# Expert rows of a mixture-of-experts stage moved through DRAM instead of through selection matmuls

## The chip, the cores and the metric

The kernel runs on one core of a Trainium2 chip. The metric is the device time of one execution in microseconds (us); lower is better. TensorE (PE, with its weight load PEld), VectorE (DVE), ScalarE (ACT), GpSimd (POOL) and SyncE (SP) run their own instruction streams and meet at semaphores. SP and POOL also issue DMAs, all of which run on the same 16 DMA engines.

## What is computed

Two layers of a hybrid model on 256 tokens of 1,024 features, in f32. Layer 0 ends in a dense feed-forward block, layer 1 in a mixture of eight experts with two chosen per token, and the output is a last RMS norm. What matters here is the expert part:

```python
def moe_swiglu(h, w_router, w1, w3, w2):
    logits = (h @ w_router).astype(jnp.float32)
    top_v, top_i = lax.top_k(logits, TOP_K)            # 2 of 8
    gates = jax.nn.softmax(top_v, axis=-1)
    combine = jnp.sum(one_hot(top_i, N_EXPERTS) * gates[..., None], axis=-2)
    out = jnp.zeros_like(h)
    for e in range(N_EXPERTS):
        out = out + combine[..., e:e + 1] * swiglu(h, w1[e], w3[e], w2[e])   # D=1024, F=3584
    return out
```

## The kernel before

All large products take each f32 weight as a high and a low part. SP loads weight tiles of 1 MB into a ring of six slots (L911). ACT copies a tile to its high part `wh` (L429), DVE subtracts to get the low part `wl` (L433), and TensorE multiplies three combinations of high and low parts (L369 for the up projections w1 and w3, L394 for the down projection w2). `wh` and `wl` have three buffers. SP may refill a slot when DVE has split it: it waits on `w_split` in `free` and walks the program in order.

In the expert part the router picks two experts per token. Each chosen pair (token, expert) gets a slot number; an expert's pairs fill blocks of 128 slots, and each block is a job. Here there are 8 jobs, known only at run time, so each engine runs a loop over jobs. A job has 14 steps (pairs of 128 hidden columns). A step is a first up half, the turn of the last step's gated values (L382), a second up half, and the down product of the step before: three stages of 12 matmuls, 3 MB of weights. A job thus reads 42 tiles, 44.04 MB. `pe_steps`, `act_steps`, `dve_steps` and `sp_ffn` hold the stages of the four engines.

A job's input columns are picked by matmul. POOL builds 0/1 matrices `sel` from compares of slot numbers by DVE (`hit`, L844 and L891), and TensorE multiplies the rows of h by them (`gather`, through L1082, 32 matmuls in f32 halves). ACT and DVE split the result into `xh` and `xl` (L740, L829). The results of a job are in banks 2 and 3; ACT copies them to `yj` (L751), and TensorE multiplies them by the transposed gate matrix `pgt` (`turn_gates`, `scatter`), DVE adds the four banks to `xT` (L836), and the accumulators are zeroed again (`zero_acc`, L421). All this stands around a job's last down product and the next job's first up halves. The last norm works on feature-major `xT`: squares on ACT, sums by matmul, root, scaling on DVE, turning back by TensorE, four copies, one store of 1 MB (L994).

The order on each engine is the order in which the code is written. POOL's share in layer 0 is a chain for another mixer, which ends with a signal and is followed by a wait for `chunk_masked` before twelve maskings (L1075).

Of the kernel before, what the change touches and what calls it, by code (L numbers as in the profile page):

```python
# [21 lines left out]
F32 = mybir.dt.float32  # L22
# [23 lines left out]
C = P  # L46
# [99 lines left out]
def program(nc, A, out):  # L146
    ctx = ExitStack()
    with ctx:
# [35 lines left out]
        xl = sb("xl", [P, KT, T], F32R)  # L184
        proj = mx_sb("proj", [P, 26, T])
# [53 lines left out]
        sel = sb("sel", [P, TT, C])  # L239
        selg = sb("selg", [P, TT, C])  # L240
        selt = sb("selt", [P, TT, C])
        hit = sb("hit", [P, 2, TT, C])
        pgt = sb("pgt", [P, T])
        rt = sb("rt", [P, T])
        jt = sb("jt", [P, 2 * MAXJOBS], I32)
        idx = sb("idx", [P, 16], U32)

# [100 lines left out]
        SCATTER = (2, 3, 5, 6)  # L348
# [36 lines left out]
        def pe_down(pe, run, m, last=False):  # L385
# [4 lines left out]
            for o in range(2 if run.moe else KT):  # L390
                for a in range(2):
                    for g, b in ((gh, 0), (gh, 1), (gl, 0)):
                        if run.moe:
                            ins = nc.tensor.matmul(bank[2 + o][:], g[:, a, 0:C], w[b][:, a, o * 512:(o + 1) * 512],  # L394
                                                   start=False, stop=False, skip_group_check=True)
# [8 lines left out]
        def pe_steps(pe, run):  # L404

            def step(m, par):
                pe_up(pe, run, m, par, 0)
                pe_turn_gated(pe, run, m - 1)
                pe_up(pe, run, m, par, 1)
                pe_down(pe, run, m - 1)  # L410

            n = run.pairs - 1
            with pe.Fori(0, n // 2) as i:
                step(2 * i + 1, 1)
                step(2 * i + 2, 0)
            if n % 2:
                step(n, 1)
# [231 lines left out]

        def hrows():  # L650
            return wide[:].rearrange("p (a b) t -> p a (b t)", a=TT)

        def pe_moe(pe, mm, turn):
# [20 lines left out]
            pe.wait_ge(sem("h_copied"), 4)  # L674
# [11 lines left out]
            def turn_gates(j):  # L686
                pe.wait_ge(sem("selg_built"), j + 1)
                for tt in range(TT):
                    turn(bank[7][:, tt * P:(tt + 1) * P], selg[:, tt], sig="gates_turned" if tt else None)

            def scatter(j):

                pe.wait_ge(sem("gates_copied"), j + 1)
                pe.wait_ge(sem("acc_copied"), 2 * j + 2)
                for b in range(4):
                    for k in range(2):
                        dt = 2 * b + k
                        mm(bank[SCATTER[b]][:, k * T:(k + 1) * T], yj[:, dt * P:(dt + 1) * P], pgt[:],
                           sig="scattered" if k else None)
# [3 lines left out]
            zero_acc((2, 3))  # L703
            run = job(0)
            pe.wait_ge(sem("x_split"), x_before(1, 2) + 2)
# [4 lines left out]
            with pe.Fori(1, n_jobs) as j:  # L710
# [3 lines left out]
                turn_gates(j - 1)  # L714
# [4 lines left out]
                scatter(j - 1)  # L719
                pe.wait_ge(sem("scatter_added"), 4 * (j - 1) + 2)  # L720
                zero_acc((2, 3))
                pe_steps(pe, nxt)
# [3 lines left out]
            turn_gates(j)  # L726
            pe_down(pe, run, last, True)
            scatter(j)

        def act_moe(act, copy, f, square):  # L730
            for b in range(4):
                act.wait_ge(sem("h_turned"), b + 1)
                copy(hrows()[:, :, b * T:(b + 1) * T], bank[b][:].rearrange("p (a t) -> p a t", a=TT), "h_copied")
            act.wait_ge(sem("gate_logit"), 1)
# [9 lines left out]
            def gates(j):  # L744
                act.wait_ge(sem("gates_turned"), j + 1)
                nc.scalar.copy(pgt[:], bank[7][:, 0:T]).then_inc(sem("gates_copied"), 1)

            def acc(j):
                act.wait_ge(sem("stage_used"), job(j).down(0, True)[0] + 1)
# [1226 lines left out]
```

## Time and profile before

| | |
|---|---|
| runs of the kernel | 1789.15 us median of 3 (1787.06 to 1795.26) |
| the profiled execution | 1791.82 us |
| its span, first to last instruction | 1789.7 us |
| mean granted TensorE clock | 0.953 |
| PE, PEld, DVE, ACT, POOL busy | 94%, 80%, 75%, 59%, 6% of the span |
| bytes read from HBM | 426.25 MB |

The span is what the trace shows; the execution's own time is 2.1 us longer. The layers' mixers and the dense block take the first 745 us, the expert jobs run from 762 to 1771 us, and the rest is the end. A row of the page's groups gives an instruction's line, engine, operation, tiles written and read, count, busy time and mean duration.

### The profile page before, as it was taken

The page shows a single profiled execution, that of the slowest core. Times are in us where ns is not written, and L with a number is a line of the kernel's source. Part 1 is how long each engine was busy: PE and PEld are TensorE (multiplying, and loading weights), DVE is VectorE, ACT ScalarE, POOL GpSimd, SP SyncE. Part 2 cuts the span into 40 slices and gives each one's busy share as a digit, 9 for nine tenths or more (in the row PEclk, how much of TensorE's full clock was granted, in tenths as well). Part 3 has the DMA queues.
Part 4 walks back from the last instruction along what each step waited for, and adds up shares of the span by engine and source line. Part 5 has one row for each costly group of instructions (what it writes and reads, how often), then busy time and mean ns, then how long its engine had stood idle before and what let it go on. Part 6 is the DMA issues. An engine that isn't in the chain of part 4 may idle for free.

```text
span 1789.7 us, 27022 instructions
## 1 busy us (share of the span) xinstructions
PE 1677.0 (94%) x9570; PEld 1429.4 (80%) x9570; DVE 1347.3 (75%) x1286; ACT 1061.1 (59%) x1039; POOL 113.7 (6%) x151
## 2 busy tenths in 40 slices
PE   6889888999798898799999999999999999999997
PEld 6778677999797775778888888888888888888886
DVE  4888455444458765678888798898888888888885
ACT  4533344344344334477777677677677677777775
POOL 1142000000004310000000000000000000000000
PEclk8989688999898995799999999999999999999999
DMA  7520034654252100489999999999999999999993
GB/s 227 156 71 25 16 102 160 208 168 136 94 165 69 65 1 21 168 274 367 326 350 368 325 346 366 317 366 358 316 366 357 327 367 341 340 367 327 354 368 119
DMA packets 327136, 427.99 MB, mean 239 GB/s; under 512 B 6848, under 2 KB 294752, under 8 KB 326960
## 3 DMA queue, kind: packets, MB, share of 16 engines
q1 hardware_dynamic: 326304, 425.28, 70.5%
q0 software_dynamic: 640, 2.00, 0.4%
q8 instruction: 33, 0.54, 0.1%
q14 instruction: 15, 0.12, 0.0%
q10 hardware_dynamic: 144, 0.05, 0.0%
HBM read 426.25 MB, written 1.05 MB: 239 GB/s over the span
## 4 chain that ended last, share of the span: by engine, by line
PE 79%; DVE 10%; ACT 5%; issue 4%; DMA 2%; SPq 0%; DVEq 0%; ACTq 0%; POOL 0%; POOLq 0%
PE bank L369 30%; PE bank L394 16%; PE bank L1082 10%; PE bank L622 7%; PE bank L372 7%; PE bank L397 4%; DMA ring<-in_moe_w 2%; ACT wh L429 2%; PE bank L382 1%; DVE wl L433 1%; PE bank L1087 1%; ACT mh L603 1%; PE bank L1348 1%; DVE proj L1671 1%; DVE ml L609 1%
## 5 line engine op out<-in xcount | busy, mean ns | idle before, releaser
L433 DVE TENSOR_TENSOR wl<-ring,wh 128x2048 fp32r<-128x2048 f32 x369 | 845.4, 2293 | 206.6 <-ACT wh L429 192.6
L429 ACT ACTIVATE wh<-ring 128x2048 fp32r<-128x2048 f32 x369 | 705.8, 1915 | 125.8 <-PE bank L394 43.5
L369 PE MATMUL bank<-wh,xh 128*128 128x512 f32 x896 | 360.5, 402 | 0.9 <-DVE xl L829 0.9
L369 PE MATMUL bank<-wh,xl 128*128 128x512 f32 x896 | 350.7, 391 | 0.0
L369 PE MATMUL bank<-wl,xh 128*128 128x512 f32 x896 | 349.2, 390 | 0.0
L369 PEld LDWEIGHTS bank<-wh,xl 128*128 128x128 f32 x896 | 168.1, 188 | 37.3
L369 PEld LDWEIGHTS bank<-wh,xh 128*128 128x128 f32 x896 | 168.2, 188 | 35.9 <-issue 3.0
L369 PEld LDWEIGHTS bank<-wl,xh 128*128 128x128 f32 x896 | 168.7, 188 | 32.3
L394 PE MATMUL bank<-wh,gh 128*128 128x512 f32 x448 | 175.3, 391 | 4.2 <-DVE gl L519 4.2
L394 PE MATMUL bank<-wh,gl 128*128 128x512 f32 x448 | 174.4, 389 | 0.0
L394 PE MATMUL bank<-wl,gh 128*128 128x512 f32 x448 | 174.3, 389 | 0.0
L622 PE MATMUL bank<-xh,mh 128*128 128x256 f32 x464 | 140.5, 303 | 33.6 <-DVE xl L577 17.6
L603 ACT ACTIVATE mh<-ring 128x1024 fp32r<-128x1024 f32 (+1 forms) x68 | 69.9, 1034 | 119.0 <-PE bank L622 118.1
L609 DVE TENSOR_TENSOR ml<-ring,mh 128x1024 fp32r<-128x1024 f32 (+1 forms) x68 | 81.3, 1207 | 78.2 <-ACT mh L603 77.2
L622 PE MATMUL bank<-xh,ml 128*128 128x256 f32 x464 | 136.6, 294 | 0.0
L622 PE MATMUL bank<-xl,mh 128*128 128x256 f32 x464 | 136.4, 294 | 0.0
L470 ACT ACTIVATE gh<-bank 128x256 fp32r<-128x256 f32 x112 | 42.9, 383 | 140.9 <-PE bank L382 140.9
L622 PEld LDWEIGHTS bank<-xh,mh 128*128 128x128 f32 x464 | 94.4, 203 | 38.4 <-DVE xl L577 18.4
L457 ACT ACTIVATE silu<-bank,const 128x256 f32<-128x256 f32 x134 | 62.4, 474 | 93.3 <-PE bank L369 52.2
L372 PE MATMUL bank<-xh,wh 128*128 128x256 f32 x352 | 100.5, 286 | 6.1 <-DVE xl L577 6.1
L394 PEld LDWEIGHTS bank<-wh,gh 128*128 128x128 f32 x448 | 84.1, 188 | 22.9 <-DVE gl L519 5.6
L372 PE MATMUL bank<-xh,wl 128*128 128x256 f32 x352 | 100.3, 285 | 0.0
(281 smaller groups left out, 2468.2 us busy)
## 6 DMA issues: line engine op xcount, KB each, us to landing
ring<-in_moe_w SPq DMA_DIRECT2D x336, 1024.0 KB, 8.2
ring<-in_ffn_w SPq DMA_DIRECT2D x33, 1024.0 KB, 5.9
ring<-in_w_in SPq DMA_DIRECT2D x24, 1024.0 KB, 5.5
ring<-in_w_out SPq DMA_DIRECT2D x8, 1024.0 KB, 5.2
ring<-in_w_in SPq DMA_DIRECT2D x2, 640.0 KB, 4.0
const<-in_const SPq DMA_DIRECT2D x1, 1200.0 KB, 14.1
proj<-in_x SPq DMA_DIRECT2D x4, 256.0 KB, 6.4
out<-wide SPq DMA_DIRECT2D x1, 1024.0 KB, 4.0
```

The source lines that it names most:

```text
L369: ins = nc.tensor.matmul(up_bank(run, par, 0)[:], x[:, 0:C], w[b][:, k], **kw)
L372: ins = nc.tensor.matmul(up_bank(run, par, item)[:, kind * T:(kind + 1) * T], w[b][:, k, at:at + P], x, **kw)
L394: ins = nc.tensor.matmul(bank[2 + o][:], g[:, a, 0:C], w[b][:, a, o * 512:(o + 1) * 512], start=False, stop=False, skip_group_check=True)
L397: ins = nc.tensor.matmul(bank[2 + o // 2][:, o % 2 * T:(o % 2 + 1) * T], w[b][:, a, o * P:(o + 1) * P], g[:, a], start=False, stop=False, ...
L429: nc.scalar.activation(o, src[0], ACT.Copy).then_inc(sem("w_high"), 1)
L433: nc.vector.tensor_tensor(split(wl[:, buf]), src[0], split(wh[:, buf]).bitcast(F32), ALU.subtract).then_inc(sem("w_split"), 1)
L457: nc.scalar.activation(silu[:, item], up_bank(run, par, item)[:, 0:T], ACT.Silu, bias=cst("zero")).then_inc(sem("silu_done"), 1)
L470: nc.scalar.activation(o, i, ACT.Copy).then_inc(sem("g_high"), 1)
L603: nc.scalar.activation(mh[:, part, :, 0:n], ring[:, slot, 4 * part:4 * part + 4, 0:n], ACT.Copy).then_inc(sem("unit_high"), 1)
L609: nc.vector.tensor_tensor(ml[:, part, :, 0:n], ring[:, slot, 4 * part:4 * part + 4, 0:n], mh[:, part, :, 0:n].bitcast(F32), ALU.subtract). ...
L622: ins = nc.tensor.matmul(o[:, c * T:(c + 1) * T], l, r, start=part == c == k == n == 0, stop=part == 1 and k == 3 and n == 2, skip_group_c ...
L1082: ins = nc.tensor.matmul(o, l, r, start=start, stop=stop)
```

## The change

1. `job_x` and `job_y` are new DRAM tensors of 16 x 128 rows of 1,024 f32 (8.4 MB each). In layer 0 POOL clears a tile and stores it over both with two DMAs, ahead of its wait for `chunk_masked`.
2. After routing, POOL stores each token's row of h twice by slot number into `job_x` (four indirect DMAs of 128 rows of 4 KB), waits for them, loads `final_norm` broadcast to 128 partitions, and loads the first job's 128 rows (`xrow`, 0.52 MB). In each pass of the job loop it loads the next job's rows, then stores `yj` to `job_y`.
3. `gather` is now eight transposes of `xrow`. `sel`, `selg`, `hit`, `pgt`, their compares, `turn_gates`, `scatter`, the adds to `xT` and the zeroing are gone; the first down product of a job starts its accumulators afresh, after a wait for `acc_copied`.
4. `xT` is turned to token rows (`xtok`, in hT's place) before the jobs: 16 transposes and four copies.
5. After the last job: store, wait, four indirect loads of 128 rows from `job_y`, four multiply-adds by the gates, then squares, root, reciprocal and scaling per half of the tokens, and two stores of 0.5 MB by SP.

```diff
-        sel = sb("sel", [P, TT, C])
-        selg = sb("selg", [P, TT, C])
...
+        xrow = sb("xrow", [P, D])
+        job_x, job_y = (nc.dram_tensor(n, (MAXJOBS * C, D), F32).ap() for n in ("job_x", "job_y"))
...
-        def pe_steps(pe, run):
-
-            def step(m, par):
+        def pe_steps(pe, run, j=0):
+
+            def step(m, par, first=False):
                 pe_up(pe, run, m, par, 0)
                 pe_turn_gated(pe, run, m - 1)
                 pe_up(pe, run, m, par, 1)
-                pe_down(pe, run, m - 1)
+                if first:
+                    wait(pe, "acc_copied", 2 * j)
+                pe_down(pe, run, m - 1, first=first)
...
             def gather(j):
 
-                pe.wait_ge(sem("sel_built"), j + 1)
+                pe.wait_ge(sem("x_loaded"), 16 * j + 16)
                 for half in range(2):
                     for d in range(4):
-                        for tt in range(TT):
-                            k = 4 * half + d
-                            mm(bank[5 + half][:, d * C:(d + 1) * C], hrows()[:, tt, k * P:(k + 1) * P], sel[:, tt],
-                               tt == 0, tt == 1, "gathered" if d == 3 and tt else None)
...
+                        k = 4 * half + d
+                        turn(bank[5 + half][:, d * C:(d + 1) * C], xrow[:, k * P:(k + 1) * P],
+                             sig="gathered" if d == 3 else None)
...
                 pe_turn_gated(pe, run, last)
                 gather(j)
-                turn_gates(j - 1)
                 pe_down(pe, run, last, True)
                 pe.wait_ge(sem("x_split"), x_before(1, 2) + 2 * j + 2)
                 pe_up(pe, nxt, 0, 0, 0)
                 pe_up(pe, nxt, 0, 0, 1)
-                scatter(j - 1)
-                pe.wait_ge(sem("scatter_added"), 4 * (j - 1) + 2)
-                zero_acc((2, 3))
-                pe_steps(pe, nxt)
+                pe_steps(pe, nxt, j)
...
             def acc(j):
                 act.wait_ge(sem("stage_used"), job(j).down(0, True)[0] + 1)
+                act.wait_ge(sem("y_stored"), 16 * j + 16)
                 for half in range(2):
                     nc.scalar.copy(yj[:, half * 512:(half + 1) * 512], bank[2 + half][:]).then_inc(sem("acc_copied"), 1)
...
         def pool_moe(pool):
...
+            pool.wait_ge(sem("zero_filled"), 16)
+            pool.wait_ge(sem("h_copied"), 4)
+            pool.wait_ge(sem("slots_ready"), 1)
+            for tt in range(TT):
                 for i in range(2):
...
+                    pool.indirect_dma_start(job_x, bass.IndirectOffsetOnAxis(ap=sidx[:, 2 * tt + i:2 * tt + i + 1], axis=0),
+                                            hrows()[:, tt], None).then_inc(sem("rows_placed"), 16)
+            pool.wait_ge(sem("rows_placed"), 32 * TT)
+
+            def load(j):
+                pool.dma_start(xrow[:], job_x[bass.ds(j * C, C), :]).then_inc(sem("x_loaded"), 16)
+
+            def store(j, sig="y_stored"):
+                pool.wait_ge(sem("acc_copied"), 2 * j + 2)
+                pool.dma_start(job_y[bass.ds(j * C, C), :], yj[:]).then_inc(sem(sig), 16)
...
+            load(0)
             n_jobs = jobs_of(pool)
             with pool.Fori(1, n_jobs) as j:
-                job_matrices(j)
+                pool.wait_ge(sem("gathered"), 2 * j)
+                load(j)
+                store(j - 1)
+            j = last_job(pool)
+            store(j, "last_stored")
+            pool.wait_ge(sem("last_stored"), 16)
+            for tt in range(TT):
+                for i in range(2):
+                    pool.indirect_dma_start(yrow(tt, i), None, job_y,
...
+                if layer == 0:
+                    settle(nc.gpsimd.memset(xrow[:], 0.0))
+                    for rows_, sig in ((job_x, "zero_filled"), (job_y, "y_stored")):
+                        pool.dma_start(rows_.rearrange("(j p) d -> p j d", p=C),
+                                       xrow[:].unsqueeze(1).broadcast_to([P, MAXJOBS, D])).then_inc(sem(sig), 16)
 
                 pool.wait_ge(sem("chunk_masked"), 4 * layer + 1)
...
-            for b in range(4):
-                act.wait_ge(sem("scatter_added"), 4 * j + b + 1)
-                square(2 * DEPTH, b)
+            for tt in range(TT):
+                act.wait_ge(sem("rows_added"), tt + 1)
+                f(hrows()[:, tt], xtok()[:, tt], ACT.Square, accum=ssq[:, tt:tt + 1])
+                f(ssq[:, tt:tt + 1], ssq[:, tt:tt + 1], ACT.Sqrt, "row_std", 1.0 / D, cst("eps_rms"))
...
+                for i in range(2):
+                    g = choice("gate")[:, i, tt:tt + 1]
+                    stt(xtok()[:, tt], yrow(tt, i), g, xtok()[:, tt], ALU.mult, ALU.add, "rows_added" if i else "dve_chain")
```

How the instructions stand, by engine. First TensorE at the start of a pass of the job loop, before the change: the turn of the last gated values, then what was `gather` (`sel`) and `turn_gates` (`selg`), then the last down product.

```order
L382 MATMUL bank<-const,gate 128x128 x2
L678 REGISTER_ALU
L1082 MATMUL bank<-sel,wide 128x128 x16
L1087 MATMUL bank<-const,selg 128x128 x2
L387 ISA
L388 REGISTER_ALU
L394 MATMUL bank<-wh,gh 128x512
```

The same place with the change (L1091 is the helper `turn`):

```order
L381 MATMUL bank<-const,gate 128x128 x2
L697 ISA
L1091 MATMUL bank<-const,xrow 128x128 x8
L386 ISA
L387 REGISTER_ALU
L393 MATMUL bank<-wh,gh 128x512
```

Eight transposes stand where 16 matmuls (each run twice in the trace, as 32) and two transposes were; the wait at L697 is now for a DMA. Further down in the same pass, before the change, the scatter and the zeroing stood between the first up halves and the step loop; with the change nothing does.

```order
L694 ISA
L1082 MATMUL bank<-pgt,yj 128x256 x8
L720 ISA
L421 MATMUL bank<-zeros 128x512 x2
L413 UNCONDITIONAL_BRANCH
```

POOL from the routing on, with the change:

```order
L877 DMA job_x<-wide,sidx 2048x1024 x4
L888 DMA fin<-in_final_norm 128x1024
L882 DMA xrow<-job_x 128x1024
L892 UNCONDITIONAL_BRANCH
L882 ISA
L885 ISA
L886 DMA job_y<-yj 128x1024
L892 COMPARE_AND_BRANCH
L901 DMA ring<-job_y,sidx 128x1024 x4
```

In the loop (from L892 to L892) the load of `xrow` stands ahead of the store of `yj`, which waits for ACT's copies; the next pass's load follows that store.

## Rows read from the trace of the kernel before

**Rows 1.** The page's part 1: busy time of each engine.

```profile
PE 1677.0 (94%) x9570; PEld 1429.4 (80%) x9570; DVE 1347.3 (75%) x1286; ACT 1061.1 (59%) x1039; POOL 113.7 (6%) x151
```

**Rows 2.** Tile `yj`: ACT's copies, two per job, first and last start.

```profile
L751 ACT COPY yj<-bank x16: 585/590/592, 885.8 to 1770.3; 128x512 f32<-128x512 f32 x16
```

**Rows 3.** Timeline of TensorE at a job boundary: start, us, what [idle before <-releaser].

```profile
1005.03 0.38 PE L382 MATMUL bank<-const,gate 128*128 128x128 f32 x2
...
1005.25 3.74 PE L1082 MATMUL bank<-sel,wide 128*128 128x128 f32 x32
...
1010.26 0.50 PE L394 MATMUL bank<-wh,gh 128*128 128x512 f32 x1 [1.06 <-DVE gl L519]
...
1018.56 3.61 PE L1082 MATMUL bank<-pgt,yj 128*128 128x256 f32 x16
...
1022.85 0.50 PE L369 MATMUL bank<-wh,xh 128*128 128x512 f32 x1
```

**Rows 4.** Timeline of ACT at the same boundary.

```profile
1005.64 1.91 ACT L429 ACTIVATE wh<-ring 128x2048 fp32r<-128x2048 f32 x1 [2.58 <-DMA ring<-in_moe_w]
...
1013.32 1.07 ACT L751 COPY yj<-bank 128x512 f32<-128x512 f32 x2 [1.64 <-PE bank L394]
```

**Rows 5.** Timeline of DVE there: the split that frees two slots.

```profile
1011.45 2.44 DVE L433 TENSOR_TENSOR wl<-ring,wh 128x2048 fp32r<-128x2048 f32 x1
```

**Rows 6.** DMA issues of 900 to 909 us and of 981 to 990: count, size, landing.

```profile
ring<-in_moe_w SPq DMA_DIRECT2D x3, 1024.0 KB, 7.6
...
ring<-in_moe_w SPq DMA_DIRECT2D x3, 1024.0 KB, 9.1
```

**Rows 7.** Stretches: us, busy of each engine, PEclk, DMA share, GB/s.

```profile
800.00:860.00 60.00, 60.00 (x272) 49.36 (x271) 53.79 (x36) 45.77 (x37) 0.00 (x0) 1.00 1.08 367
1012.00:1016.00 4.00, 4.00 (x19) 3.34 (x18) 1.89 (x1) 2.68 (x3) 0.00 (x0) 1.00 0.23 53
1032.00:1036.00 4.00, 4.00 (x21) 3.25 (x20) 3.93 (x3) 2.94 (x3) 0.00 (x0) 1.00 0.39 122
754.00:760.00 6.00, 5.75 (x31) 5.78 (x32) 4.47 (x13) 0.60 (x1) 2.01 (x4) 0.58 0.01 3
135.00:180.00 45.00, 42.16 (x350) 36.47 (x347) 37.88 (x45) 15.06 (x27) 12.28 (x11) 1.00 0.08 25
```

**Rows 8.** DMA of 1708 to 1790 us: GB/s in 40 slices of 2.05 us.

```profile
GB/s 400 371 349 348 391 382 349 348 381 392 350 346 368 401 353 349 360 406 354 349 350 404 198 410 32 0 0 0 0 0 0 0 0 0 0 0 0 0 340 172
```

**Rows 9.** Timeline before the first job: DVE's last slot number, then TensorE.

```profile
752.27 0.17 DVE L823 TENSOR_REDUCE rt<-rt 128x2 f32<-128x16 f32 x1
...
754.25 6.09 PE L1082 MATMUL bank<-sel,wide 128*128 128x128 f32 x32 [4.36 <-POOL sel L891]
...
761.75 0.50 PE L369 MATMUL bank<-wh,xh 128*128 128x512 f32 x1 [0.88 <-DVE xl L829]
```

**Rows 10.** POOL's DMA issues (1,024 and 128 rows), then landing by the page's part 6.

```profile
23.71 0.90 POOL L1007 DMA_DIRECT2D router<-in_moe_router  x1
25.29 0.59 POOL L1013 DMA_DIRECT2D wukv<-in_mla_w_ukv  x1
...
wukv<-in_mla_w_ukv POOLq DMA_DIRECT2D x2, 256.0 KB, 3.6
```

**Rows 11.** Timeline of POOL in layer 0 around the place of the clearing.

```profile
128.76 0.40 POOL L1066 COPY hk<-hk 128x256 f32<-128x256 f32 x1
139.92 1.53 POOL L1075 TENSOR_TENSOR mtm<-rw,const 128x512 f32<-128x512 f32 x1 [10.76 <-DVE rw L1677]
```

**Rows 12.** The end: ACT's last copies, DVE's scaling, the store's issue and landing.

```profile
1769.82 1.07 ACT L751 COPY yj<-bank 128x512 f32<-128x512 f32 x2 [3.31 <-PE bank L394]
...
1780.58 3.25 DVE L1694 SCALAR_TENSOR_TENSOR hT<-xT,par,rstd 128x256 f32<-128x256 f32 x8
...
1785.35 0.39 SPq L994 DMA_DIRECT2D out<-wide  x1
...
out<-wide SPq DMA_DIRECT2D x1, 1024.0 KB, 4.0
```

More of the change, by code:

```diff
@@ L383, in pe_turn_gated, with pe_down @@
                 ins.then_inc(sem("g_turned"), 1)
-        def pe_down(pe, run, m, last=False):
+        def pe_down(pe, run, m, last=False, first=False):
             stage, buf = run.down(m, last)
@@ L394, in pe_down @@
                             ins = nc.tensor.matmul(bank[2 + o][:], g[:, a, 0:C], w[b][:, a, o * 512:(o + 1) * 512],
-                                                   start=False, stop=False, skip_group_check=True)
+                                                   start=first and a == 0 and g is gh and b == 0, stop=False,
+                                                   skip_group_check=True)
                         else:
@@ L409, in step @@
                 pe_up(pe, run, m, par, 1)
-                pe_down(pe, run, m - 1)
+                if first:
+                    wait(pe, "acc_copied", 2 * j)
+                pe_down(pe, run, m - 1, first=first)
             n = run.pairs - 1
+            if run.moe:
+                step(1, 1, True)
+                with pe.Fori(0, n // 2) as i:
+                    step(2 * i + 2, 0)
+                    step(2 * i + 3, 1)
+                return
             with pe.Fori(0, n // 2) as i:
@@ L725, in pe_moe, with act_moe @@
             pe_turn_gated(pe, run, last)
-            turn_gates(j)
             pe_down(pe, run, last, True)
-            scatter(j)
-        def act_moe(act, copy, f, square):
+        def act_moe(act, copy, f):
             for b in range(4):
@@ L733, in act_moe @@
                 copy(hrows()[:, :, b * T:(b + 1) * T], bank[b][:].rearrange("p (a t) -> p a t", a=TT), "h_copied")
+            for b in range(4):
+                act.wait_ge(sem("xm_turned"), b + 1)
+                copy(xtok()[:, :, b * T:(b + 1) * T], bank[b][:].rearrange("p (a t) -> p a t", a=TT), "xm_copied")
             act.wait_ge(sem("gate_logit"), 1)
@@ L765, in act_moe @@
                 up(0, 0, 0, 1)
-                gates(j - 1)
                 acc(j - 1)
@@ L884, in dve_moe @@
             dve_gated_low(dve, run, last)
[L885 to L902 removed]
+            dve.wait_ge(sem("fin_in"), 16)
@@ L991, in _ @@
                 sp_ffn(job(j), w1, w3, w2, e * D, e * FE, 0)
-            sp.wait_ge(sem("out_ready"), KT // 2)
-            sp.dma_start(out[0].rearrange("(a p) d -> p a d", p=P),
-                         wide[:].rearrange("p (a b) t -> p a (b t)", a=TT)).then_inc(sem("out_stored"), 16)
-            sp.wait_ge(sem("out_stored"), 16)
+            for tt in range(TT):
+                sp.wait_ge(sem("out_ready"), tt + 1)
+                sp.dma_start(out[0][tt * P:(tt + 1) * P, :], hrows()[:, tt]).then_inc(sem("out_stored"), 16)
+            sp.wait_ge(sem("out_stored"), 16 * TT)
         @block.gpsimd
@@ L1429, in _ @@
             pe_moe(pe, mm, turn)
-            norm(2 * DEPTH)
-            for k in range(KT):
-                pe.wait_ge(sem("hT_ready"), 2 * DEPTH * KT + k + 1)
-                for tt in range(TT):
-                    turn(bank[k // 2][:, tt * T + k % 2 * P:tt * T + (k % 2 + 1) * P], hT[:, k, tt * P:(tt + 1) * P],
-                         sig="out_turned" if k % 2 and tt else None)
         @block.scalar
@@ L1657, in _ @@
                     act_ffn_dense(act)
-            act_moe(act, copy, f, square)
-            root(2 * DEPTH)
-            for b in range(4):
-                act.wait_ge(sem("out_turned"), b + 1)
-                copy(wide[:].rearrange("p (a b) t -> p a (b t)", a=TT)[:, :, b * T:(b + 1) * T],
-                     bank[b][:].rearrange("p (a t) -> p a t", a=TT), "out_ready")
+            act_moe(act, copy, f)
         @block.vector
```

83 lines of the change are left out of this document (26 added, 57 removed).

## The prediction

> **What bounds the kernel now.** The page's first part gives TensorE 94% of the span and DVE 75% [rows 1], which reads as "TensorE is the limit, so matmuls taken off it are time gained". I then asked how often a job ends: the first copies of `yj` start at 885.8 us and the last at 1770.3, eight jobs, so seven periods of 126.4 us [rows 2]. I next looked at one boundary on TensorE. The reader sees 3.6 us of gathering, a wait of 1.06 us for `gl`, and 3.6 us of scatter with a wait and the zeroing behind it, until the first stage of the step loop at 1022.85 [rows 3].
>
> The third view is the DMA one, and it changes the picture. In the middle of a job TensorE has no gap and the DMA engines no idle time either: 367 GB/s over 60 us, share above 1 [rows 7]. TensorE takes a step (three stages of 12 matmuls at 0.227 us and two transposes) in 8.43 us. The time from issue to landing of the three loads of a step grows from 7.6 us at 900 to 9.1 us at 981 [rows 6]: 1.5 us in nine steps, so the loads need about 0.17 us more than TensorE's step, 8.60 us for 3 MB, 2.87 us per tile. At the end of a job ACT waits for a tile: 2.58 us at 1005.64 [rows 4]. A job's 42 tiles need 42 x 2.87 = 120.4 us of the 126.4. Only 6 us of a period are free on the DMA engines, and two dry spells account for nearly all: of 1012 to 1016 some 3.2 us are empty (share 0.23 against 1.08 when full) and of 1032 to 1036 some 2.6 us [rows 7]. So TensorE and the weight stream are almost even, and the boundary is where the stream catches up.
>
> **The job boundaries.** TensorE first. The gather goes from 3.6 us to eight transposes at 0.11 us (the pair of row L382 takes 0.22 us until the next starts), 0.9 us [rows 3]. Turning the gates, 0.22 us, and all from 1018.56 to 1022.85, 4.3 us, go [rows 3]. But the down product behind the gather waits for `gl` on DVE, which already ends the gather's time; less cover there gives the wait back. I count 4.3 us saved at a boundary where ACT waited for a tile, 5 us elsewhere. DVE loses its adds and compares, POOL its matrices; neither was ahead of TensorE.
>
> Now the stream. It gets two transfers per job, `xrow` and `yj`, of 0.52 MB each in rows of 4 KB. The slices near the end alternate between 350 and 400 GB/s [rows 8], as tiles with 1 KB rows and with 4 KB rows follow each other, so I price 4 KB rows at 400 GB/s: 1.31 us each, 2.6 us per job (no DMA out of a loop writes DRAM here; the bounds are nothing, if they fit wholly into dry time, and 5.2 us, if they disturb the other queue as much again). Weights and rows now need 123.0 us per job. The second dry spell closes: TensorE arrives 4 to 5 us sooner while the refills are no sooner. The first does not: it ends when SP sees the split of the new job's second tile, 1013.9 [rows 5], which no removed instruction stood in front of. And the store comes late for it: ACT's copies end at 1014.4 [rows 4], POOL issues the store and behind it the next `xrow`, so both queue with SP's refill. I keep 3.1 us of idle: 123.0 + 3.1 = 126.1 against 126.4. Seven boundaries: **-2 us**. Lower bound 2.0 us of idle, as a stream that is late runs dry later: 125.0, -10 us. With 5.2 us for the two transfers: 128.7, +16 us. The waits on `x_loaded` and `y_stored` cost nothing: both were issued a whole job earlier.
>
> The Trainium skill (HBM Reference, section Specifications (TRN2)) says that a core streaming alone measures about 425 GB/s, bounded by its DMA engines. By that a job's 44.04 MB would take 103.6 us and TensorE's whole saving would be gained. The row says 367, and the growing landing time says that this is the limit here; the sum goes by the row.
>
> **The entry.** Today the last slot number is out at 752.44 and the first expert matmul runs at 761.75, 9.3 us later [rows 9]. With the change: a cast, 0.2 us; four indirect stores of 2.1 MB in all. An issue takes 0.6 to 0.9 us on POOL, and 256 KB land in 3.6 us, of which 0.65 are data at 400 GB/s, so 3.0 us are fixed [rows 10]. 752.7 + 3.0 + 5.2 of data = 760.9. Then `final_norm` is issued ahead of the load, 0.6 us, and both move 1 MB: 761.5 + 3.0 + 2.6 = 767.1. Eight transposes at the lower clock level, twice 0.11 each, then the second half's `xh` and `xl`: 770.8, so +9.0 us. The granted clock in the gather's stretch is 0.58, near its lower level of 1.2 GHz, after TensorE had been idle 4.4 us [rows 7, 9]; it would be idle for 13 us now, and I add 1.5 us for a first stage at that level (0 to 4). A compare of slots that holds up the first `gl` by 0.8 us goes. Together **+10 us**; +6 if the four stores overlap better, +18 if an indirect DMA costs POOL three times a direct one. The turning of `xT` lies beside all this.
>
> The skill (DMA: Bandwidth & Descriptors, section Anatomy of one DMA) gives 2.0 us fixed plus bytes at 436 GB/s; by it the placing and the load would take 3 us less in all, and this term would be +7 us.
>
> **The clearing.** It writes 16.8 MB, 42 us at 400 GB/s, from 130 us on, where the engines are empty but for one tile (25 GB/s over 135 to 180) [rows 7]. POOL is free from 129.2 to 139.9 [rows 11]. A clear of the tile (about 1 us) and two issues; 1,024 rows cost 0.90 us against 0.59 for 128 [rows 10], so 2,048 some 1.3 us. **0 us**, covered by POOL's wait; if POOL had to wait for the writes, the maskings would come up to 32 us later (130 + 42 against 140).
>
> **The end.** Today 18.8 us run from the end of the copies at 1770.9 to the span's end [rows 12]. With the change: store, 3.0 + 1.3, until 1775.2; four indirect loads, the first pair there 3.0 + 2.6 later, the second 2.6 more, at 1783.4; two multiply-adds of 1,024 columns at four times 0.41 us less their starts, 1.2 us each (DVE scales 256 in 0.41 us [rows 12]), 1785.8; square 1.2, root 0.3, reciprocal and scaling 1.4, 1788.7; a store of 0.5 MB in 4.0 less 1.3 [rows 12] plus 0.4 of issue, 1791.8. **+2.5 us**, from -1 to +10.
>
> **The sum.** -2 + 10 + 0 + 2.5 = +10.5 us. Against the profiled execution's own 1791.82: 1802.3. That execution lies 2.7 us above the median, so for the median 1789.15 + 10.5, **1800 us**. A measurement of this kernel tells about 0.5%, 9 us, from no change: below 1780 is faster, above 1798 slower.
>
> **The rivals.**
> - *The transfers decide, as forecast*: 45%. For it: landing times that grow through a job and a wait for a tile at its end.
> - *The rows slip into the dry time*: the period falls to 125.0, the entry costs 8: 1789.15 - 10 + 8 + 2.5 = 1790. For it: 6 us are free per job and only 2.6 are wanted. Against: both come when the dry spell ends. 22%.
> - *The stream has room after all*, the other side. If the tiles are late only because they are asked for late, or a second queue fills gaps between packets, TensorE sets the period and each boundary gives 4.3 to 5 us: -32 + 12.5 = 1769 or 1770. It decides if the weights could move in under 118 us per job, 373 GB/s. For it: single slices above 400. Against: 366 GB/s whenever the queue is full, and ACT's wait. The skill's rule above is this case. 13%.
> - *The rows cost double*, by alternating with tiles: +16 instead of -2, 1818. 12%.
> - *POOL is held by the clearing*: +32, 1832. Against: the issue times hardly grow with rows. 8%.
>
> **How the numbers follow.** Below 1780: the third rival and a tail of the second, 17%. Within 1780 to 1798: the rest of the second, and two fifths of the forecast, whose entry may be cheaper: 35%. Above 1798: 48%. The range 1779 to 1823 leaves out most of the third and the fifth rival.
>
> **What would show it.** In the trace after: a period of `yj` near 126 us though the scatter is gone; gaps on TensorE in every step, about 0.2 us, with ACT waiting for tiles all through jobs 1 to 7; one dry spell per boundary instead of two; TensorE busy below 94%; the first expert matmul near 771; the first masking at 139.9. A period under 122 us with no waits for tiles would prove me wrong on the stream, a masking late in layer 0 on the clearing.

## The result and the profile after

The changed kernel takes 1803.42 us (median of 6 runs, 1797.94 to 1804.83) against 1790.13 us before (6 runs, 1786.57 to 1795.26): ratio 1.0063, 95% interval 1.0041 to 1.0084. It is slower by 0.6%, a small difference but one that the interval keeps apart from none, and 3.4 us above the forecast of 1800. Its profiled execution took 1804.3 us, with a span of 1802.7.

The page's part 1, against [rows 1]:

```profile
PE 1641.2 (91%) x9202; PEld 1380.1 (77%) x9202; DVE 1305.3 (72%) x1227; ACT 1057.8 (59%) x1031; POOL 113.6 (6%) x147
```

TensorE is busy for 36 us less and the kernel is 13 us longer. The copies of `yj` against [rows 2]:

```profile
L748 ACT COPY yj<-bank x16: 586/589/594, 897.5 to 1779.4; 128x512 f32<-128x512 f32 x16
```

Seven periods of 126.0 us in the mean where there were seven of 126.4, and the first copy comes 11.7 us later. TensorE at the same boundary, against [rows 3]:

```profile
1018.10 1.04 PE L1091 MATMUL bank<-const,xrow 128*128 128x128 f32 x8
1022.99 0.76 PE L393 MATMUL bank<-wh,gh 128*128 128x512 f32 x1 [3.86 <-DVE gl L527]
```

The gather takes 1.0 us instead of 3.7, there is no scatter, and 3.86 us of waiting stand where 1.06 did. ACT shows why, against [rows 4]: its program has the split of the new job's first tile ahead of `gh`, and the tile comes 2.46 us after ACT is ready for it.

```profile
1018.37 1.91 ACT L437 ACTIVATE wh<-ring 128x2048 fp32r<-128x2048 f32 x1 [2.46 <-DMA ring<-in_moe_w]
1020.18 0.37 ACT L478 ACTIVATE gh<-bank 128x256 fp32r<-128x256 f32 x1
...
1027.71 1.07 ACT L748 COPY yj<-bank 128x512 f32<-128x512 f32 x2 [4.38 <-PE bank L393]
```

The list of waits gives `ACT wh` waiting for a tile 85 times and 47.8 us in all; before it was 7 times and 11.8 us.

```profile
ACT wh L437 <- DMA ring<-in_moe_w: 47.8, 85, 2.6
```

The wait is not all. TensorE runs the last down product behind it at a lower granted clock. The first of these stretches is that product with the change, the second the same product before (columns as in [rows 7]):

```profile
1022.99:1027.71 4.72, 4.72 (x14) 3.77 (x15) 3.34 (x3) 0.34 (x2) 0.00 (x0) 0.64 0.40 153
1010.26:1013.32 3.06, 3.06 (x13) 2.55 (x14) 3.01 (x3) 1.42 (x3) 1.40 (x3) 1.00 0.53 210
```

It takes 4.7 us in place of 3.1. This is so at five of the changed kernel's seven boundaries between jobs and at none before. So 2.8 us more of waiting and 1.7 us of lower clock take back 4.5 us of what the matmuls saved there.

The stretches, against [rows 7] (us, busy of each engine, PEclk, DMA share, GB/s):

```profile
800.00:860.00 60.00, 60.00 (x271) 48.77 (x270) 52.62 (x36) 45.60 (x36) 0.00 (x0) 1.00 1.07 366
1004.00:1008.00 4.00, 4.00 (x19) 3.29 (x18) 2.71 (x3) 3.46 (x4) 0.00 (x0) 1.00 0.64 218
1012.00:1016.00 4.00, 4.00 (x20) 3.28 (x19) 3.35 (x3) 2.67 (x3) 0.00 (x0) 1.00 1.09 362
1024.00:1028.00 4.00, 4.00 (x14) 3.20 (x13) 2.33 (x2) 0.29 (x1) 0.00 (x0) 0.69 0.28 88
1032.00:1036.00 4.00, 3.98 (x18) 2.92 (x17) 3.99 (x4) 2.68 (x3) 0.00 (x0) 1.00 1.03 375
```

The dry spell behind the boundary is left (1024 to 1028, 3.0 of 4 us empty, counting 1.08 as full), and the stretch at 1032, which was nearly two thirds empty, is full. A second, shorter one stands ahead of this first boundary (1004 to 1008, 1.6 us empty) and is all but gone at the later ones. Over the first six periods the stream moves 45.1 MB per job where it moved 44.05, and a period holds 4.0 us more than these bytes need at 367 GB/s, where it held 6.7: 2.7 us of idle time are gone, and the rows, 2.9 us at that rate, take them.

What ends the dry spell is DVE's split of the new job's second tile:

```profile
1024.05 2.28 DVE L441 TENSOR_TENSOR wl<-ring,wh 128x2048 fp32r<-128x2048 f32 x1
```

It starts behind DVE's other work, without a wait, so it hangs on the late tile and not on TensorE's slower product.

The entry, against [rows 9]: the four placing stores, the load, the transposes, the first expert matmul.

```profile
753.36 0.17 DVE L819 TENSOR_REDUCE rt<-rt 128x2 f32<-128x16 f32 x1
753.57 0.17 DVE L820 CAST sidx<-rt 128x4 uint32<-128x4 f32 x1
754.65 1.11 POOL L877 DMA_INDIRECT job_x<-wide,sidx  x1 [106.85 <-DVE sidx L820]
...
758.63 0.96 POOL L877 DMA_INDIRECT job_x<-wide,sidx  x1 [0.30 <-issue]
762.95 0.59 POOL L888 DMA_DIRECT2D fin<-in_final_norm  x1 [3.36 <-DMA job_x<-wide,sidx]
763.55 0.56 POOL L882 DMA_DIRECT2D xrow<-job_x  x1
768.55 1.97 PE L1091 MATMUL bank<-const,xrow 128*128 128x128 f32 x8 [15.77 <-DMA xrow<-job_x]
...
771.98 0.76 PE L368 MATMUL bank<-wh,xh 128*128 128x512 f32 x1 [1.46 <-issue]
```

From the last slot number to the first expert matmul it is 18.6 us, where it was 9.5. The clearing stands in POOL's free time and the masking behind it waits for DVE as before and starts 0.5 us later, against [rows 11]:

```profile
129.77 0.95 POOL L1068 MEMSET xrow<- 128x1024 f32 x1
131.02 1.23 POOL L1070 DMA_DIRECT2D job_x<-xrow  x1 [0.30 <-POOL xrow L1068]
...
140.39 3.09 POOL L1079 TENSOR_TENSOR mtm<-rw,const 128x512 f32<-128x512 f32 x2 [6.98 <-DVE rw L1669]
```

The span's growth of 13.0 us is then: entry and first job together +10.7 (from the last slot number to the first copy 133.5 us before, 144.2 now), seven periods -2.6, the end +3.9 (22.7 us from the last copy to the span's end against 18.8), and 1.1 that had come before the last slot number. I count that last one as no part of the change: over the profiled executions of all kernels here that number comes out between 747.3 and 755.5 us.

### The profile page after: what moved, and what is told of

It is laid out like the page before. It is cut to its first block, busy times and chain, and to the rows that moved or that the text cites. A ratio compares the mean times of both kernels' runs of the same rounds, so it can differ in the third digit from the quotient of the medians.

```text
span 1802.7 us, 26185 instructions
## 1 busy us (share of the span) xinstructions
PE 1641.2 (91%) x9202; PEld 1380.1 (77%) x9202; DVE 1305.3 (72%) x1227; ACT 1057.8 (59%) x1031; POOL 113.6 (6%) x147
## 4 chain that ended last, share of the span: by engine, by line
PE 67%; DVE 12%; DMA 9%; ACT 5%; issue 5%; SPq 1%; POOL 0%; DVEq 0%; ACTq 0%; POOLq 0%
PE bank L368 25%; PE bank L393 12%; PE bank L1086 9%; DMA ring<-in_moe_w 8%; PE bank L630 7%; PE bank L371 7%; DVE wl L441 4%; PE bank L397 4%; ACT wh L437 2%; PE bank L381 1%; PE bank L1091 1%; DVE ml L617 1%; ACT mh L611 1%; PE bank L1352 1%; DVE proj L1663 1%
## 5 line engine op out<-in xcount | busy, mean ns | idle before, releaser
L437 ACT ACTIVATE wh<-ring 128x2048 fp32r<-128x2048 f32 x369 | 705.8, 1916 | 161.9 <-DMA ring<-in_moe_w 47.8
L368 PE MATMUL bank<-wh,xh 128*128 128x512 f32 x896 | 370.2, 413 | 6.0 <-DVE wl L441 4.3
L371 PE MATMUL bank<-xl,wh 128*128 128x256 f32 x352 | 100.3, 285 | 0.0
```

What stands on the lines that cost most here:

```text
L368: ins = nc.tensor.matmul(up_bank(run, par, 0)[:], x[:, 0:C], w[b][:, k], **kw)
L371: ins = nc.tensor.matmul(up_bank(run, par, item)[:, kind * T:(kind + 1) * T], w[b][:, k, at:at + P], x, **kw)
L437: nc.scalar.activation(o, src[0], ACT.Copy).then_inc(sem("w_high"), 1)
```

## The experiments

**Theory:** the weight stream moves at most about 367 GB/s, a job is as long as its bytes need plus the time in which the stream runs dry at the boundary, and what the change takes off TensorE there is mostly exchanged for row transfers. **Rivals:** rows cost nothing; TensorE (or the order of ACT and DVE) sets the period. All results are below. The period is that between `yj` copies, last less first over seven, from one profiled execution each; a copy behind a product at the lower clock comes 1.6 us late, which moves such a mean by 0.2 us. Each ratio is to runs of the kernel before that were made beside it, with medians of 1790.1 to 1791.7 us.

| kernel | us (runs) | ratio to before, 95% | yj copies | period |
|---|---|---|---|---|
| before | 1790.13 (6) | 1 | 885.8 to 1770.3 | 126.4 |
| changed | 1803.42 (6) | 1.0063 (1.0041 to 1.0084) | 897.5 to 1779.4 | 126.0 |
| 1 changed, no row transfers | 1789.49 (10) | 0.9983 (0.9967 to 0.9998) | 897.6 to 1763.0 | 123.6 |
| 2 changed, rows doubled | 1819.61 (4) | 1.0161 (1.0120 to 1.0202) | 897.2 to 1794.5 | 128.2 |
| 3 changed, half `w2` | 1784.57 (10) | 0.9963 (0.9946 to 0.9980) | 896.2 to 1760.0 | 123.4 |
| 4 before, half `w2` | 1784.78 (10) | 0.9971 (0.9953 to 0.9990) | 880.1 to 1761.8 | 126.0 |
| 5 changed, loads exchanged | 1809.50 (4) | 1.0111 (1.0084 to 1.0139) | 892.5 to 1782.0 | 127.1 |
| 6 before, loads exchanged | 1793.11 (10) | 1.0008 (0.9991 to 1.0025) | 885.3 to 1768.9 | 126.2 |
| 7 changed, `gl` first | 1807.23 (6) | 1.0102 (1.0081 to 1.0123) | 893.4 to 1782.2 | 127.0 |
| 8 changed, zeros at the entry | 1807.61 (4) | 1.0087 (1.0053 to 1.0121) | 904.7 to 1785.9 | 125.9 |
| 9 mixture, loads exchanged | 1783.40 (8) | 0.9959 (0.9939 to 0.9979) | 883.8 to 1755.0 | 124.5 |
| 10 mixture | 1793.32 (12) | 1.0016 (1.0006 to 1.0027) | 881.7 to 1765.9 | 126.3 |
| 11 changed, tiles in halves | 1775.93 (6) | 0.9922 (0.9904 to 0.9941) | 894.3 to 1749.3 | 122.1 |
| 12 mixture, tiles in halves | 1765.74 (5) | 0.9852 (0.9834 to 0.9871) | 887.7 to 1742.8 | 122.2 |

### 1 and 2: what a job's row transfers cost

```diff
-            with pool.Fori(1, n_jobs) as j:
-                pool.wait_ge(sem("gathered"), 2 * j)
-                load(j)
-                store(j - 1)
```

(with the waits on `x_loaded` and `y_stored` at 16; one load and one store are left.) And doubled:

```diff
+                pool.dma_start(spare[:], job_x[bass.ds(j * C, C), :]).then_inc(sem("spare_in"), 16)
...
+                pool.dma_start(job_z[bass.ds(j * C, C), :], yj[:]).then_inc(sem("z_stored"), 16)
```

> The changed kernel without the row transfers of the job loop: `xrow` is loaded once, `yj` is stored once, after the last job. It leaves out the load of every later job's rows and the storing of seven results, so its output is not the reference's; every other instruction stays. Stream theory (weights 120.4 us per job, rows 2.6, one dry spell): the 1.04 MB per job go, so the period of `yj` falls from 126.0 to about 123.3 us and the whole from 1803 to about 1784 us. Rival, rows for nothing (they slip into the dry time, or a second queue moves them in gaps): period 126.0, total within 3 us of 1803. Rival, rows cost double: period near 121, total near 1768.

> The changed kernel with both row transfers of a job doubled: `xrow`'s rows are loaded a second time into a spare tile, and `yj` is stored a second time to another DRAM buffer, so 2.1 MB move per job in place of 1.04. Taking both away gave 2.4 us per job (period 126.0 to 123.6). If rows cost their bytes on a full stream: +2.4 to 2.7 us per job, period 128.4 to 128.7, total near 1821. Rival, they cost by disturbing the tiles while they run or by their descriptors and waits rather than by bytes, so that the second of a pair behind the first is cheap: under +1 us per job. Rival, POOL's extra issues (about 0.9 us each) hold up the `xrow` load until the next gather waits for it: period over 130.

Measured: 123.6 us without them, 128.2 with twice as many, so 2.4 us per job for the first 1.05 MB and 2.2 for the second. By the medians it is 13.9 and 16.2 us over seven periods, 2.0 and 2.3 each, and the total without rows is 1789.5, above the 1784 I had expected. Rows cost about their bytes, at 440 to 480 GB/s as a difference of periods; free rows and rows at double price both fall.

### 3 and 4: the stream relieved, in both kernels

```diff
-                         w2[bass.ds(row2 + m * T, T), :].rearrange("(a p) d -> p a d", p=P))
+                         w2[bass.ds(row2 + m * T, n * P), :].rearrange("(a p) d -> p a d", p=P))
```

(`n` is 1 in expert jobs: only the first 128 of a tile's 256 rows are loaded.)

> The changed kernel, in whose expert jobs each `w2` tile loads only its first 128 rows (0.5 MB in place of 1 MB; the second half of the slot holds what was there, so the output is not the reference's). No instruction of an engine changes; a job's weights are 36.7 MB in place of 44.04, some 103 us of stream. Stream theory: the stream no longer bounds it, TensorE does, and the time that the change takes off TensorE at a boundary (4.3 to 5 us) shows: period 120 to 122.3 us against 126.0, total 1760 to 1777. Rival, the saving on TensorE is given back by waits for `gl` and the splits, whatever the stream does: period 124.5 to 126.

> The same halving of the `w2` tiles in the kernel before the change (its output is not the reference's for the same reason). Stream theory: before the change TensorE sets nearly all of the period and the stream costs only the wait for a tile at a job's end, so the period falls little, from 126.4 to 125 to 125.8 us, total 1780 to 1787. With the run of the changed kernel beside it the difference of the two periods is then 3.3 to 5 us in favour of the change, where with whole tiles it is 0.4. Rival, the stream bounded the kernel before as well: period 121 to 123, and the two kernels stay as close as they are with whole tiles.

Measured: the kernel before falls by 0.4 us per job, the changed one by 2.6. TensorE set nearly all of the kernel before (six of its relieved periods are 126.2 to 126.3 us), the stream sets the changed one. But the changed kernel stops at 123.4, above my 120 to 122.3 (and its total of 1784.6 above my 1777): relieved of the stream it gains 2.6 us on the kernel before, not 4.3 to 5. Its TensorE still waits twice at a boundary, for `gl` and for a split of the third tile pair, which SP asks for only after the new job's second split:

```profile
1014.08 0.50 PE L393 MATMUL bank<-wh,gh 128*128 128x512 f32 x1 [1.51 <-DVE gl L527]
1033.46 0.49 PE L368 MATMUL bank<-wh,xh 128*128 128x512 f32 x1 [2.19 <-DVE wl L441]
```

ACT stands ahead of the second:

```profile
1029.05 1.92 ACT L437 ACTIVATE wh<-ring 128x2048 fp32r<-128x2048 f32 x1 [2.66 <-DMA ring<-in_moe_w]
```

In the relieved kernel before no wait of TensorE is listed from 1000 to 1040: gather, scatter and zeroing had covered them. At three of the relieved changed kernel's eight last down products the granted clock is 0.64 and they take 4.7 us. And the two relieved kernels take the same time (0.9963 and 0.9971): seven times 2.6 us about pay for the entry and the end.

### 5 and 6: two loads exchanged

```diff
+                if run.moe:
+                    down(1, 1, True, 0)
+                    up(2, 0, False, 2)
+                else:
                     up(2, 0, False, 2)
                     down(1, 1, True, 0)
```

> The changed kernel with two of SP's loads in the other order: at a job's start the `w2` tile of its second down product is issued ahead of the two tiles of its third up product. That slot is free as soon as the previous job's last tile is split, so the transfer no longer stands behind a wait for the new job's second split; the same bytes move in all. Stream theory: 2 to 2.7 us of the dry spell at each boundary (now share 0.28 over 1024 to 1028 us) are filled, so the period goes from 126.0 to 123.3 to 124.8 us and the total from 1803 to 1785 to 1795 us. Rival, the dry spell is covered anyway because TensorE or the order of the splits sets the boundary: period 126.0, total 1803.

> The same exchange of two loads in the kernel before the change. There TensorE has 94% of the span and two dry spells stand at each boundary. If TensorE sets the boundary there, as I read it (the weights need 120.4 of 126.4 us, so there is slack in the stream): the period stays within 0.5 us of 126.4 and the total within 3 us of 1790. If the stream already bounds the kernel before as well, as the growing landing times and the wait of ACT for a tile would have it: period about 124, total about 1774. A value between says that the wait for a tile at a job's end is all that the stream costs there (2.6 us per boundary at most).

Before the change: nothing, as expected. In the changed kernel my forecast had the wrong sign, 1.1 us per job slower. The dry spell is filled, and two others open behind it (stretches of the changed kernel with loads exchanged):

```profile
1016.00:1020.00 4.00, 3.66 (x16) 3.05 (x17) 3.68 (x4) 1.19 (x3) 0.00 (x0) 1.00 1.04 405
1037.00:1041.00 4.00, 3.02 (x9) 2.37 (x10) 4.00 (x4) 2.46 (x2) 0.00 (x0) 0.72 0.47 184
1049.00:1053.00 4.00, 4.00 (x20) 3.26 (x19) 3.92 (x3) 2.93 (x3) 0.00 (x0) 1.00 0.64 238
```

The `w2` tile that now fills the spell is not wanted yet, and the up tiles that are come behind it. TensorE then stands for their split:

```profile
1037.98 0.49 PE L368 MATMUL bank<-wh,xh 128*128 128x512 f32 x1 [4.47 <-DVE wl L441]
```

ACT had been idle 4.96 us ahead of that split. The row names TensorE's down product as what released it, but in the changed kernel the same split starts 2 us before that product does, so I read it as the tile. Late splits free slots late, and the stream runs dry further on. In the mixture (9 against 10) the same exchange gains 1.9 us per job, and 9.9 us in all; its 1783.4 lies just above the 1767 to 1781 expected. I have no account of the opposite sign that a run tells apart.

### 7: `gh` and `gl` ahead of the next job's split

```diff
                 act_end_a(act, run)
-                up(0, 0, 0, 0)
                 act_gated_high(act, run, last)
+                up(0, 0, 0, 0)
```

(and on DVE alike)

> The changed kernel with two steps in another order at a job's boundary, on ACT and DVE alike: the last gated values' `gh` and `gl` are made ahead of the split of the next job's first tile, and not behind it. In the changed kernel TensorE waits there 2.5 to 3.9 us for `gl`, which is its longest wait, because ACT first waits for that tile. Stream theory: the tile comes no earlier, so the wait only moves behind the last down product, and the period stays between 125.3 and 126.3 us, total 1798 to 1806. Rival, the order of ACT and DVE is what gives TensorE's saving back at the boundary: period 122 to 123.5 us, total 1776 to 1786.

Measured: 127.0 us, 1807.2 in all. The longest wait in TensorE's list goes, and as long a one comes back in two pieces behind it:

Timeline of TensorE:

```profile
1023.00 0.49 PE L368 MATMUL bank<-wh,xh 128*128 128x512 f32 x1 [2.02 <-DVE xl L826]
1040.38 0.49 PE L368 MATMUL bank<-wh,xh 128*128 128x512 f32 x1 [1.64 <-DVE wl L441]
```

The order of ACT and DVE was not what took TensorE's saving. The granted clock still falls behind these waits (0.57 from 1024 to 1028 us), so this run does not price the clock. That it costs 1 us, outside my 125.3 to 126.3, is in line with splits of the new tiles that come later, but not shown.

### 8: TensorE kept busy at the entry

```diff
+            for _ in range(60):
+                zero_acc((4,))
             gather(0)
```

> The changed kernel with 60 matmuls of zeros into an unused bank ahead of the first job's gathering, so that TensorE is not idle for the 15 us in which rows are placed and loaded. My theory of the entry: the first stage of 12 matmuls runs 0.43 us each in place of 0.23 because the granted clock had fallen to the lower level during the idle time; with the clock kept up it gains 2.5 us at the entry and about 1 us at the gathering's transposes (1.97 us for eight, 1.04 at the boundaries), so the first copy of `yj` starts 2 to 3.5 us earlier than 897.5 and the total falls from 1803 to about 1800, within what can be told apart only in the trace. Rival, the stream sets the end of the first job too: the matmuls are faster but the first `yj` stays within 0.5 us of 897.5.

A miss. The matmuls of zeros were too long: 0.36 us each, so they ended at 774.7, 6 us after the rows were there. And they did not do what they were put in for. The granted clock was still 1.00 when they began. It fell under them to 0.50 (1.2 GHz) between 756 and 757 us, as in the changed kernel, where TensorE stood idle there. The first two of these stretches are of the kernel with zeros, the third of the changed kernel:

```profile
753.00:756.00 3.00, 3.00 (x15) 1.29 (x14) 0.88 (x6) 2.68 (x4) 1.11 (x1) 1.00 0.46 179
757.00:760.00 3.00, 3.00 (x8) 0.99 (x7) 1.89 (x9) 0.00 (x0) 2.12 (x3) 0.50 0.88 356
757.00:760.00 3.00, 0.00 (x0) 0.00 (x0) 1.76 (x9) 0.00 (x0) 1.98 (x3) 0.50 0.88 355
```

The first expert stage was as slow as without them (0.43 us from one matmul to the next). What a full clock would give at the entry stays unmeasured.

### 9 and 10: rows gathered on TensorE, results through DRAM

The mixture keeps `compare_slots`, `sel` and the gathering matmuls of the kernel before, and drops `job_x`, its clearing, placing and loads:

```diff
-                load(j)
+                build(j)
                 store(j - 1)
...
-                pe.wait_ge(sem("x_loaded"), 16 * j + 16)
+                pe.wait_ge(sem("sel_built"), j + 1)
```

> A mixture: rows are gathered on TensorE with the slot matrix `sel` as before the change (no placing, no load of `xrow`, slots compared on DVE, `sel` built on POOL), results go through DRAM by slot as in the change (no scatter, no gates on TensorE, last norm token-major), and the loads are exchanged as in the run on SP's order. One row transfer per job is left. Stream theory: period about 122.5 to 124.4 us, the entry as before the change (first expert matmul about 9 us earlier than in the changed kernel), the end as in the change: 1789.2 + 2 (part of the entry that had shifted) + 4 (end) - 7 x 2 to 4 = 1767 to 1781 us, under both kernels. If TensorE sets the boundary instead: gather 3.6 us against 0.9, so period 2.7 us above that of the changed kernel with exchanged loads.

> The mixture without the exchange of loads: rows gathered on TensorE with `sel` as before, results through DRAM and the token-major norm as in the change. It undoes one part of the change, the placing and loading of rows. The exchange of loads cost 1.1 us per job in the changed kernel (127.1 against 126.0), and with it the mixture had a period of 124.5 us and 1783 us in all. If that cost is the same here: period 123.4, total near 1776. If the exchange was neutral in the mixture, as in the kernel before: period 124.5, total near 1783. The entry is expected as before the change (some 8 to 9 us from the last slot number to the first expert matmul, against 18 with the change), the end as with it (22.7 us after the last copies against 18.8). If it were the results' part that costs the time and not the rows' part, the total would be at or above 1803.

From the last slot number to the first expert matmul it is 9.0 us in both, against 18.6: the entry's cost is the placing and loading of rows alone. The end is the changed kernel's. Without the exchange the period was 126.3 where I had expected 123.4 to 124.5. It moves one row transfer less than the changed kernel and takes as long per job, so its dry time is the longer one (126.3 less about 121). The mixture beats the changed kernel by 10 us, and not by its period.

### 11 and 12: tiles loaded in halves

```diff
+                        for part in range(2):
...
+                                sp.wait_ge(sem("w_split"), run.stages + (n - 1 + part))
+                            for slot, w in zip(UP[par], (w1, w3)):
+                                sp.dma_start(slot_of(slot)[:, 4 * part:4 * part + 4],
+                                             w[bass.ds(row13 + T * 2 * part, D // 2), bass.ds(m * T, T)]
+                                             .rearrange("(k p) n -> p k n", p=P)).then_inc(sem(f"w_ready_{par}{part}"), 16)
```

> The changed kernel in which the two tiles of an up product are loaded in halves that match the splits: each split reads rows 0 to 511 or 512 to 1023 of both `w1` and `w3`, so four loads of 0.5 MB are issued in place of two of 1 MB, the first pair as soon as the first split of the tiles before is done, and a split waits only for its own pair. The bytes stay. The dry spell at a boundary (now some 3 us at 1024 to 1028 us) ends at present when the second split of the new job is done; with halves its refill starts one split earlier, 2.5 to 3.7 us. Stream theory: the period falls towards 123.0 us (weights and rows without a dry spell), 123.2 to 124.8, total 1784 to 1795. Rival, four smaller loads cost the stream more than they give (each pair's rows are the same 1 KB): period 126 or above, total 1803 or more.

> The mixture (rows gathered on TensorE, results through DRAM) with the up tiles loaded in halves. One row transfer per job is left, so weights and rows need 121.7 us per job; TensorE needs some 121 to 122 at least. Stream theory: period 121.7 to 123, total 1763 to 1775, under both kernels by 15 us or more. Rival, loads in halves give nothing: 123.4 to 124.5 us and 1776 to 1783, as for the mixture with whole tiles.

The changed kernel falls to 122.1 us per job and 1775.9 us, below my 123.2 to 124.8. Its stream is never dry; two whole stretches of a job:

```profile
895.00:1015.00 120.00, 118.50 (x535) 96.15 (x534) 105.67 (x72) 92.89 (x73) 1.07 (x2) 1.00 1.08 367
1015.00:1137.00 122.00, 120.51 (x539) 95.78 (x538) 106.06 (x73) 94.34 (x74) 1.07 (x2) 1.00 1.08 368
```

and ACT now waits for tiles in every step, none of them long:

```profile
ACT wh L437 <- DMA ring<-in_moe_w: 109.7, 215, 0.7
```

This bears the theory out most directly: bytes and rate unchanged, dry time gone, 3.9 us per job gained. The earlier refill and the split that starts on half the bytes were not tried apart. TensorE's wait for `gl` is also down to 1.3 to 1.5 us at the boundaries, and the product behind it runs at a granted clock of 1.00 and takes 3.1 to 3.2 us at all of them; no run gives one without the other. The Trainium skill (HBM Reference, section Specifications (TRN2)) says about 425 GB/s for a core alone; the rows say 366 to 368 over long stretches in which the queue is full, so the measurement decides, for this mix of tiles.

The mixture with halves is the fastest kernel here, 1765.7 us, 1.5% under the kernel before. It has half the row bytes and still the same period; its TensorE is busy all but 0.2 us of the stretch below and six of its periods are all 122.4 us, so I read TensorE as what sets it. No run relieves its stream to show it.

```profile
1010.00:1132.00 122.00, 121.79 (x564) 100.10 (x563) 107.55 (x75) 92.45 (x74) 1.28 (x2) 1.00 1.07 365
```

## Why the prediction was right

**The boundaries, -2 us: measured -2.6.** The mechanism held: the stream bounds, rows cost their bytes, one dry spell closes and the other stays. That the number fits is in part luck, on two counts. I spread the gain evenly over seven periods; in fact the first six take 761.3 us together where they took 760.3, and the last one, behind which no job follows, 120.1 where it took 123.7. So between jobs about nothing is gained and the last period gives 3.6 us. With the stream relieved in both kernels it gives 4.1. And the terms were each a little off and cancel. Rows: 2.0 to 2.4 us per job, not 2.6 (experiments 1 and 2). Weights and rows without dry time: 122.1 (experiment 11), not 123.0, so the weights were 0.5 to 0.7 us too dear as well. Dry time: 126.0 - 122.1 = 3.9 us, not 3.1.

**TensorE's saving of 4.3 to 5 us: wrong, and without effect here.** With the stream relieved it is 2.6 (experiments 3 and 4). I had said that less cover gives the wait for `gl` back, and then did not subtract all of it; the second wait, for tiles asked for too late, and the lower clock behind a long wait (1.7 us per down product) I did not see. That spoils the rival "the stream has room": its 1769 would have been about 1785. The clearest sign of which bound held was therefore not in that price but in the waits: 85 of ACT for tiles, and steps of 8.59 us (six of them between the turns of gated values at 943.39 and 994.93) where they were 8.43; the sum had 8.60.

**The entry, +10: measured +10.7.** The first expert matmul came 9.1 us later after the last slot number, as forecast, but by two errors that cancel. I had nothing between the cast and the first store, and 0.9 us pass there; the stores themselves took 8.3 us from the first issue to that of `fin`, against my 8.2. The loads took less: 5.6 us from the issue of `fin` to landed `xrow`, against 6.2. The stage at half the clock cost 2.5 us and not 1.5, and the 0.8 us of the first `gl` went: the first job took 125.5 us in place of 124.0.

**The clearing, 0: right.** The rival of POOL held by it falls.

**The end, +2.5: measured +3.9.** The terms as I gave them add up to 20.9 us from the copies on, 2.1 more than the 18.8 of before and not 2.5; measured are 22.7. The store was right: 4.2 us from the end of the copies to the first indirect load, against 4.3. The Trainium skill's rule (DMA: Bandwidth & Descriptors, section Anatomy of one DMA), 2.0 us and the bytes at 436 GB/s, gives an estimate of 3.2 us for 0.5 MB, and the trace agrees: 3.2 us from the start of the store's issue to the load that waits for it. The step that was off is the one behind it, from the first indirect load to the last multiply-add: 12.1 us against 10.6. The first pair of loads is there after 6.8 us and not 5.6, and DVE then runs all four multiply-adds in one piece, 5.3 us, where I had counted two of 1.2 behind the second pair. POOL's 1.3 us per issue are no other price than the bytes: 0.52 MB at 400 GB/s. What follows took 6.5 us against 6.0.

```profile
1784.18 1.01 POOL L901 DMA_INDIRECT ring<-job_y,sidx  x1 [2.62 <-DMA job_y<-yj]
...
1788.04 0.95 POOL L901 DMA_INDIRECT ring<-job_y,sidx  x1 [0.31 <-issue]
...
1790.97 5.27 DVE L1669 SCALAR_TENSOR_TENSOR hT<-ring,rt,hT 128x1024 f32<-128x1024 f32 x4 [15.21 <-DMA ring<-job_y,sidx]
```

**The sum.** +10.5 forecast, +13 in the profiled pair, of which 1.1 is not the change.

## What to carry to other kernels

An engine at 94% and a weight stream at 95% of the same period are two bounds, and work taken off the engine is worth only what the stream's dry time allows: price the period as bytes over the full rate plus dry time, and look for what ends each dry spell. Refill at the grain at which slots are read (a half tile freed, a half tile asked for); moving a later load forward fills the same spell with bytes that nobody waits for and can open another behind it. A longer wait of the engine can cost twice, as here, where the product behind it ran at a granted clock of 0.64. Rows that pass through DRAM once before a loop cost their fixed latencies in a chain (some 9 us here), and the longest wait in a list need not be one whose removal gains.

## What was not expected

- The same exchange of two loads costs 1.1 us per job in the changed kernel, nothing in the kernel before, and gains 1.9 in the mixture. Why the sign turns stays open.
- Sixty matmuls of zeros (one row by 512), back to back for 21.9 us, did not hold the granted clock: it fell from 1.00 to 0.50 under them at the same place as without them, and rose only under the expert matmuls behind them.
- An indirect DMA of 128 rows of 4 KB holds POOL for 0.95 to 1.11 us and 0.30 us pass before the next, against 0.54 to 0.59 us for a direct one of 0.5 MB.
